# A seven-product scheme for the down product of seven turns, and weight sums made by GpSimd in the middle stage

## The reference

```python
D_MODEL = 1024
D_FF = 4 * D_MODEL
    xn = rmsnorm(x, norm1_g)
    proj = xn @ w_in
    ...
    mixed = jax.nn.sigmoid(gate_a) * y_a + jax.nn.sigmoid(gate_b) * y_b
    h = x + mixed @ w_o
    f = jnp.square(jax.nn.relu(rmsnorm(h, norm2_g) @ w_up)) @ w_down
    return h + f, new_buf_a, new_buf_qkv, S_new
```

## Time and profile before

| what | value |
|---|---|
| median of 3 runs | 1758.71 us (1756.45 to 1761.66) |
| profiled execution, span | 1754.7 us |
| TensorE busy | 1725.3 us, 98% |
| VectorE busy | 993.6 us, 57% |
| ScalarE busy | 566.7 us, 32% |
| GpSimd busy | 124.1 us, 7% |
| mean granted TensorE clock | 0.996 |
| DMA | 126.48 MB, mean 72 GB/s |

### The profile page before, as it was taken

One profiled execution on the slowest core, in us unless ns is written; L12 is line 12 of the kernel. 1 busy time (PEld: TensorE's weight loads), 2 busy tenths in 40 slices (PEclk: granted clock), 3 DMA queues, 4 the chain that ended last, 5 costly groups with the idle time before them and its releaser, 6 DMA issues.

```text
span 1754.7 us, 25319 instructions
## 1 busy us (share of the span) xinstructions
PE 1725.3 (98%) x10557; PEld 1620.3 (92%) x10557; DVE 993.6 (57%) x1457; ACT 566.7 (32%) x1134; POOL 124.1 (7%) x109
## 2 busy tenths in 40 slices
PE   6999999999999999999999999999999999999998
PEld 6999989998999999999988899999998888999987
DVE  5566547665411142322162877777789666667667
ACT  5222224444211111111141544444344232333334
POOL 1000023433000000000000300000002000000001
PEclk9999999999999999999999999999999999999999
DMA  6011111000511111021060133333333212232313
GB/s 195 25 39 46 54 43 48 1 25 27 167 37 49 37 37 49 25 61 49 13 240 1 57 109 108 101 97 96 97 96 97 86 59 73 84 97 84 96 61 120
DMA packets 119757, 126.48 MB, mean 72 GB/s; under 512 B 5178, under 2 KB 96007, under 8 KB 119644
## 3 DMA queue, kind: packets, MB, share of 16 engines
q1 hardware_dynamic: 119644, 124.87, 23.0%
HBM read 115.21 MB, written 9.64 MB: 71 GB/s over the span
## 4 chain that ended last, share of the span: by engine, by line
PE 82%; DVE 3%; issue 1%; ACT 1%; POOL 0%; POOLq 0%; DVEq 0%; ACTq 0%
PE ps L1898 26%; PE ps L2697 21%; PE ps L2685 20%; PE ps L2634 6%; PE ps L1381 2%; PE ps L1404 1%; PE ps L1462 0%; PE ps L1477 0%; PE ps L1486 0%; PE ps L1440 0%; PE ps L1320 0%; PE ps L1471 0%; DVE ft L1136 0%; PE ps L2646 0%; DVE ti L1168 0%
## 5 line engine op out<-in xcount | busy, mean ns | idle before, releaser
L2697 PE MATMUL ps<-w_hi,hid_hi 128*128 128x512 f32 x576 | 224.6, 390 | 1.4 <-DVE rows L2476 1.4
L1898 PE MATMUL ps<-xn_hi,g_hi 128*128 128x384 f32 x672 | 225.0, 335 | 0.0
L1898 PE MATMUL ps<-xn_lo,g_hi 128*128 128x384 f32 x672 | 224.5, 334 | 0.0
L1898 PE MATMUL ps<-xn_hi,g_lo 128*128 128x384 f32 x672 | 224.5, 334 | 0.0
L2697 PE MATMUL ps<-w_hi,hid_lo 128*128 128x512 f32 x576 | 224.3, 389 | 0.0
L2697 PE MATMUL ps<-w_lo,hid_hi 128*128 128x512 f32 x576 | 224.1, 389 | 0.0
L2685 PE MATMUL ps<-x_half,w_hi 128*128 128x320 f32 (+1 forms) x832 | 193.8, 303 | 0.3 <-DVE xn_hi L2420 0.3
L2476 DVE TENSOR_TENSOR rows<-ps,rows 128x512 f32<-128x512 f32 x144 | 99.3, 690 | 121.2 <-PE ps L2697 120.9
L2177 ACT CAST w_hi<-ff_raw 128x1024 fp32r<-128x1024 f32 x112 | 116.6, 1055 | 141.7 <-PE ps L2697 141.7
L2685 PE MATMUL ps<-x_half,w_lo 128*128 128x320 f32 (+1 forms) x512 | 154.9, 302 | 0.0
L2378 DVE TENSOR_TENSOR w_lo<-ff_raw,w_hi 128x1024 fp32r<-128x1024 f32 x112 | 136.6, 1220 | 31.4 <-ACT w_hi L2177 30.5
(11 more groups left out here) (308 smaller groups left out, 3367.3 us busy)
## 6 DMA issues: line engine op xcount, KB each, us to landing
ff_raw<-in_w_up SPq DMA_DIRECT2D x64, 512.0 KB, 4.4
ff_raw<-in_w_down SPq DMA_DIRECT2D x32, 512.0 KB, 3.7
s<-in_w_down SPq DMA_DIRECT2D x32, 512.0 KB, 3.6
g_raw<-in_w_in SPq DMA_DIRECT2D x28, 512.0 KB, 3.8
w_raw<-in_w_in SPq DMA_DIRECT2D x16, 512.0 KB, 3.9
rows<-in_x_prompt SPq DMA_DIRECT2D x9, 512.0 KB, 6.4
wo_raw<-in_w_o SPq DMA_DIRECT2D x8, 512.0 KB, 3.7
out<-out SPq DMA_DIRECT2D x8, 512.0 KB, 2.6
```

What stands on the lines that cost most here:

```text
L1898: last = nc.tensor.matmul(ps[:, ORDER[n % 8], 0:NW], a[:, u % 3, w], x[:, c, rows_of(g)], start=(c == 0 and m == 0), stop=(c == ks - 1 and ...
L2697: last = nc.tensor.matmul(ps[:, 6 + n % 2, :], x[:, k, at], y[s][:, w], start=(first and k == ks[0] and m == 0), stop=((not first or len(k ...
```

## The change

In turns 8 to 14, that is seven turns of the second row group (`squeezed`), the down product is a seven-product scheme too. The hidden block of 640 rows is taken as 256 rows on top, one middle tile of 128 rows and 256 rows below. Top and bottom are multiplied in seven products (`DOWNS`), each of two tiles x 6 matmuls of 512 columns; the middle tile is plain, four pieces of 6 matmuls (`middle_row`). VectorE makes four sums of hidden blocks (`hidden_sum`), and nine remainders of forms (`rest_form`) in place of eight of blocks. Products that belong to several outputs stay in their PSUM bank, and the next is summed on top of them after the bank has been added to `rows`: 16 additions (`evict`) in place of 10, and TensorE waits for an addition before it goes on in that bank. Turn 15 and the first group keep the plain down product. The weights of these turns are eight units in place of four, four of them sums of quarters of w_down (T1 to T4).

`weight_sum` is gone from all turns. The sums of w_up quarters (S1 to S4) and of w_down quarters are made once, for both groups, in the middle stage: 32 sets (`SETS`), for each of which SyncE loads four pieces of 256 KB into ff_piece (`prep_load`), GpSimd makes four sums in place, each waiting for the one before (`prep_sums`), and SyncE stores the four results in DRAM (`prep_store`, ff_sums). The pieces are single buffers: the loads of a set wait for the stores of the one before. One set is stored and one loaded in each pass of the loop that loads the units of the middle stage. The feed-forward loads are one ring of five slots (`load_unit`), in the order in which the units are used, 11 a turn and 15 in the seven turns, in place of 8. Joins, squarings, copies and casts of hidden blocks are done two blocks at a time.

```diff
--- before.py
+++ after.py
+        prep = [self.at("ff_piece", [P, 512], F32, self.mem.spare + n * 2048) for n in range(4)]
+        self.ff_sums = nc.dram_tensor("ff_sums", [NFC, 8, P, D], F32).ap()
+        prep_in, prep_out, before_prep = z_in[1], z_in[0], 32
...
+        def prep_load(sp, n):
+            c, down, half = n // 4, n // 2 % 2, n % 2
+            if n:
+                sp.wait_ge(prep_out, before_prep + 64 * n)
+            else:
+                sp.wait_ge(self.rule.wx_done, H)
+                for f in range(2):
+                    sp.wait_ge(z_in[f], before_prep)
+            for j, piece in enumerate(prep):
+                row, col = divmod(j, 2)
+                if down:
+                    sp.dma_start(piece[:, :], down_view[:, 4 * c + 2 * row + half, col * 512:(col + 1) * 512]
...
+        def prep_store(sp, n):
+            c, down, half = n // 4, n // 2 % 2, n % 2
+            sp.wait_ge(prep_made, 4 * n + 4)
+            for piece, j in zip(prep, (0, 2, 3, 1) if down else (1, 3, 2, 0)):
+                sp.dma_start(self.ff_sums[c, 4 * down + j, :, half * 512:(half + 1) * 512], piece[:, :]
+                             ).then_inc(prep_out, 16)
+
+        def prep_sums(pool, n):
+            p11, p12, p21, p22 = [piece[:, :] for piece in prep]
+            tensor = nc.gpsimd.tensor_tensor
+            pool.wait_ge(prep_in, before_prep + 64 * n + 64)
+            if n // 2 % 2:
+                tensor(p11, p12, p11, ALU.subtract).then_inc(prep_made, 1)
+                pool.wait_ge(prep_made, 4 * n + 1)
+                tensor(p12, p22, p12, ALU.subtract).then_inc(prep_made, 1)
+                pool.wait_ge(prep_made, 4 * n + 2)
+                tensor(p22, p22, p11, ALU.subtract).then_inc(prep_made, 1)
+                pool.wait_ge(prep_made, 4 * n + 3)
...
             for u in range(3, NU):
                 load(sp, u)
+                if u >= 4:
+                    prep_store(sp, u - 4)
+                if u < 3 + SETS:
+                    prep_load(sp, u - 3)
...
             sp.wait_ge(tails_stored, 32)
+            sp.wait_ge(prep_out, before_prep + 64 * SETS)
             closing.sync(sp)
         def gpsimd(pool):
+            for n in range(SETS):
+                prep_sums(pool, n)
             closing.gpsimd(pool)
...
+        UPS = ("U11", "U12", "S2", "S1", "S3", "S4", "U22")
+        UD = len(UPS)
+        plain = ("B11", "B21", "B12", "B22")
+        squeezed = lambda t: NFC <= t < TURNS - 1
+
+        DOWNS = (("a11", "B11"), ("s1", "T1"), ("s2", "T2"), ("a12", "B21"), ("s3", "T3"), ("s4", "B22"), ("a22", "T4"))
+        squeezed_units = (("B11", "T1", "T2", "B21", "T3", "B22", "T4"),
+                          ("B11", "T1", "T2", "B21", "T3", "B22", "B12", "T4"))
...
+        ff_at = (t0 + 24576, t0 + 28672, t0 + 8192, t0 + 20480, spare + 4096)
+        SLOTS = len(ff_at)
...
+        ROW = {"B11": 0, "T1": 1, "T2": 0, "B21": 0, "T3": 1, "B22": 0, "T4": 1}
+        COL = {"B11": 0, "T1": 1, "T2": 1, "B21": 0, "T3": 1, "B22": 1, "T4": 0}
+        DOWN_BANK = {"B11": 6, "T1": 0, "T2": 6, "B21": 2, "T3": 6, "B22": 0, "T4": 6}
+        FRESH = ("B11", "T1", "B21")
...
+            def load_unit(t, j):
+                n, name, c = number(t, j), kinds(t)[j], t % NFC
+                if n >= SLOTS:
+                    sp.wait_ge(lo_done, NU + n - SLOTS + 1)
...
-            def weight_sum(t, n):
-
-                tensor = nc.vector.tensor_tensor
-                if n == 1:
-                    dve.wait_ge(raw_ready[0], 32 + 16 * (2 * t + 1))
-                    dve.wait_ge(raw_ready[1], 32 + 16 * (t + 1))
...
+            def hidden_sum(t, n):
...
+                if n == 1:
+                    dve.wait_ge(relu_sq, squares_of(t) + 3)
+                    ins = tensor(s1, a21, a22, ALU.add)
+                if n == 2:
+                    dve.wait_ge(form_sum, sums_made(t) + 1)
+                    ins = tensor(s2, s1, a11, ALU.subtract)
+                if n == 3:
+                    ins = tensor(a21, a11, a21, ALU.subtract)
+                if n == 4:
+                    dve.wait_ge(form_sum, sums_made(t) + 2)
+                    dve.wait_ge(kept_squared, squeezed_before(t) + 1)
+                    ins = tensor(s4, a12, s2, ALU.subtract)
...
                 rest(t, UD + 1)
+                if squeezed(t):
+                    g = group(t)
+                    join(t, 2)
+                    relu_square(t, 2)
+                    for n in (1, 2, 3):
+                        hidden_sum(t, n)
+                    rest_form(t, "s1")
+                    rest_form(t, "a22")
+                    hidden_sum(t, 4)
+                    rest(t, UD + 2)
+                    if g:
+                        rest_form(t, "mid0")
+                    rest_form(t, "s2")
+                    evict_pair(t, "B11")
+                    evict_pair(t, "T1")
+                    rest(t, UD + 3)
+                    rest_form(t, "a12")
+                    if g:
+                        rest_form(t, "mid1")
+                    evict_pair(t, "T2")
+                    rest(t, UD + 4)
+                    rest_form(t, "s3")
+                    rest_form(t, "s4")
+                    rest(t, UD + 5)
+                    evict_pair(t, "B21")
+                    if g:
+                        evict(t, "mid", 1)
+                        evict_pair(t, "T3")
+                        rest(t, UD + 6)
+                        rest(t, UD + 7)
+                        evict_pair(t, "B22")
+                        rest(t + 1, 0)
+                        evict(t, "mid", 3)
+                    else:
+                        evict_pair(t, "T3")
+                        rest(t, UD + 6)
+                        evict_pair(t, "B22")
+                        rest(t + 1, 0)
+                    rest(t + 1, 1)
+                    evict_pair(t, "T4")
+                    continue
                 rest_hidden(t, 1)
                 join(t, 2)
...
+            def down_product(t, form_name, name):
+                weights_split(t, name)
+                form_split(t, form_name)
+                if name == "B11":
+                    pe.wait_ge(summed, sums(t))
+                if name == "T1":
+                    pe.wait_ge(joined, 3 * t + 3)
+                for x in range(2):
+                    if name in ("T2", "T3", "T4"):
+                        pe.wait_ge(summed, evicted(t, {"T2": "B11", "T3": "T2", "T4": "T3"}[name], x))
+                    if name == "B22":
+                        pe.wait_ge(summed, evicted(t, "T1", x))
+                    down_piece(t, form_name, name, x, DOWN_BANK[name] + x, name in FRESH, True)
+
+            def middle_row(t, n):
+
+                name, k = (("B11", 0), ("B21", 1), ("B22", 1), ("B12", 0))[n]
+                weights_split(t, name)
+                form_split(t, f"mid{k}")
+                if n == 0:
+                    pe.wait_ge(kept, 4 * t + 4)
+                down_piece(t, f"mid{k}", name, 0, 4 + n // 2, n % 2 == 0, n % 2 == 1)
 
 
...
+                if squeezed(t):
+                    for form_name, name in DOWNS:
+                        down_product(t, form_name, name)
+                        if group(t) and name in ("T1", "B21"):
+                            middle_row(t, int(name == "B21"))
+                        if group(t) and name == "B22":
+                            middle_row(t, 2)
+                            middle_row(t, 3)
```

More of the change, by code:

```diff
@@ new lines, in close @@
+        two = lambda *names: [(n, x) for n in names for x in range(2)]
+        PIECES = (two("B11", "T1", "T2", "B21", "T3", "B22", "T4"),
+                  two("B11", "T1") + [("mid", 0)] + two("T2", "B21") + [("mid", 1)] + two("T3", "B22") +
+                  [("mid", 2), ("mid", 3)] + two("T4"))
+        EVICTS = [[x for x in pieces if x not in (("mid", 0), ("mid", 2))] for pieces in PIECES]
+        FREED = ({n: (n, 1) for n in squeezed_units[0]},
+                 {**{n: (n, 1) for n in squeezed_units[1]}, "B11": ("mid", 0), "B21": ("mid", 1), "B22": ("mid", 2),
+                  "B12": ("mid", 3)})
@@ L1949, in close @@
+        kinds = lambda t: UPS + (squeezed_units[group(t)] if squeezed(t) else plain)
+        first_unit = [0]
+        for t in range(TURNS):
+            first_unit.append(first_unit[-1] + len(kinds(t)))
+        TOTAL = first_unit[TURNS]
+        number = lambda t, j: first_unit[t] + j
         unit = lambda t, j: NU + number(t, j)
+        index = lambda t, name: kinds(t).index(name)
         slot = lambda t, j: number(t, j) % 4
-        downs = lambda t: sum(2 * tiles_of(n) for n in range(t))
@@ L1954, in close @@
-        ff_at = (t0 + 24576, t0 + 28672, t0 + 8192, t0 + 20480)
-        r21, r22, r12, r11 = [unit_at("ff_raw", F32, a) for a in ff_at]
-        pieces = lambda a: a[:, :].rearrange("p (k c) -> p k c", c=512)
-        s1 = self.at("s1", [P, 2, 800], F32, const + 5120)[:, :, 0:512]
-        s2 = self.at("s2", [P, 2, 8704], F32, base + 53248)[:, :, 0:512]
```

(8 more changed lines are left out.)

392 lines of the change are left out of this document (228 added, 164 removed).

## The result

The changed kernel takes 1869.7 us (median of four runs, 1863.3 to 1878.7), against 1757.6 us for the kernel before (median of four, 1753.5 to 1761.7): a ratio of 1.065, with a 95% interval of 1.061 to 1.069. It is slower, as forecast, but by twice the forecast amount: 1813.3 us was the prediction and 1852 us its upper end. Measured again beside later runs, the ratio was 1.059 (1.055 to 1.062). All ratios are of fast executions; the only one left out for its state is an execution of 3434.4 us of the later run without sums. The profiled execution took 1863.3 us, with a span of 1860.6 us.

The account below looks back on a forecast made before the run. TensorE's own time was taken as the bound. Span 1754.7 + 75.0 (set chain) - 19.0 (seven turns) - 1.4 (turn 7) = 1809.3 us; the median, 4.0 us above the span, gives 1813.3 us, range 1764 to 1852 us.

Parts of the forecast that it names:

- one chain of 32 T: Middle stage: 32 sets in sequence on SyncE's queue, w_o loaded only after the last store; shift 75.0 us.
- T: Middle stage: cycle of one set, loads landed, sums made, stores landed; 15.3 us predicted, no shift at 12.96 us.
- Rival (c): Middle stage: more GpSimd-VectorE meetings or slower landings, T = 16.6 us, 1855 us; chance 11%.
- the landing of the four loads: Middle stage: 1 MB of a set in four loads of 256 KB lands in mean 5.1 us.
- The bounds: Parts of a set's cycle: loads 3.6 to 5.7 us, stores 3.6 to 5.4, sums 4.4 to 7.8; together 11.7 to 19.0.
- The stores: Middle stage: a set's four stores land in 3.9 us, 2.7 for half and 1.3 for the other half.
- The sums and the lock: Middle stage: four GpSimd sums 5.3 us a set, plus 0.9 us for meetings with VectorE's two-input SBUF instructions.
- The seven turns: Turns 8 to 14: twelve fewer matmuls each, 2.72 us a turn, 19.0 us in all; VectorE 40.1 of 49.1 us.
- rival (d): Turns 8 to 14 don't get shorter because VectorE's strict order holds TensorE up: 1832 us; chance 5%.
- Turn 7: Removed weight sums end TensorE's waits for late additions of the down product there: 1.4 us gained.
- The signs named in advance: Trace signs: sets 15.3 us apart, first w_o load about 948 us, g_lo waits about 65 us, turns 49.1 us apart.
- The rival on the other side: Middle stage: the sets fit, T at or under 12.96 us, giving 1738.3 us, faster; chance 6%.

Follow-up runs that it names:

- the later run without sums: Changed kernel with GpSimd's sums removed, each set's four pieces loaded and stored again unsummed ("no sums" in the table): 1738.6 us, ratio 0.989.
- late weight load: Changed kernel, but the next unit's 512 KB weight load is issued only when the set's four loads have landed: 1822.8 us, ratio 1.040.
- one buffer, fewer requests: Changed kernel with late weight load, w_down sets loaded by one request and every set stored by one: 1813.8 us, ratio 1.033.
- plain down product: Changed kernel with sets still made, but all turns of the second row group take the plain down product: 1880.2 us, ratio 1.073.
- two buffers: Changed kernel with each set cut into two halves of 256 columns, a buffer each in the same 8 KB: 1748.8 us, ratio 0.997.
- two buffers, fewer requests: Kernel of two buffers with two loads and one store per half set instead of four and four: 1734.4 us, ratio 0.989.

## Why the prediction was wrong in size

**The place and the mechanism were right.** The prediction put the whole loss in one chain of 32 T on SyncE's queue, with its formula: 1738.3 us plus 32 (T - 12.96). With the T that each run shows, it gives:

| kernel | T, us | by the formula | measured |
|---|---|---|---|
| changed kernel | 16.90 | 1864 | 1869.7, 1860.3 |
| late weight load | 15.66 | 1825 | 1822.8 |
| one buffer, fewer requests | 15.27 | 1812 | 1813.8 |
| plain down product | 16.81 | 1862 + 18.4 = 1880 | 1880.2 |
| two buffers | 13.38 | 1752 | 1748.8 |
| two buffers, fewer requests | 12.27 | 1738 | 1734.4 |
| no sums | 11.74 | 1738 | 1738.6 |

Within 6 us in each (under T = 12.96 us the formula gives 1738 us throughout). So what failed is T: 16.9 against 15.3 us, 32 x 1.6 = 51 us, which is what the spans differ by from the forecast (105.9 against 54.6). That these agree so closely is in part luck: the first set started 3.8 us earlier than forecast, the fourth w_lo ended 1.5 us later behind the last store, and 2.4 us less were gained behind it. The other 5 us of the 56 between the medians is that the profiled execution was the fastest of its four. Rival (c), "more meetings, or landings like the slower ones", with T = 16.6 us and 1855 us, came nearest; it had 11%, and of its two reasons the landings were the right one.

**The step that failed: the landing of the four loads**, put at 5.1 us, was 6.1. I took it from two loads of 512 KB, with the next pair issued 2.7 us behind the first load, and added 0.5 us for the shorter runs of w_up. In the changed kernel loads of w_up and of w_down landed alike (6.10 and 6.18 us), and with the late weight load they were 0.2 us apart (5.90 and 5.68). The kernel before, behind the pair at 876.82 us:

```profile
879.54 1.50 SPq L2067 DMA_DIRECT2D wo_raw<-in_w_o  x2
```

Two parts of what was missing are shown. For w_down the same megabyte in four requests takes 0.5 us longer than in one (5.68 against 5.18 us on average), and the next unit's 512 KB, issued directly behind the set's loads (2.0 us after the first), adds 0.35 us (6.14 against 5.79). What stays open is why one request took 5.18 us where the two of the row took 4.8. The second part was in the code of the change for all to see: the prediction looked at what stands behind a wait in the queue, but not at what stands behind a transfer. The bounds named 5.7 us as the slow end, which was too low too: it came from a ratio of speeds, with no neighbour in it. The effect goes both ways; the weight loads land later as well (median us from issue to landing),'s loads in the kernel before against the kernel after:

```profile
g_raw<-in_w_in SPq DMA_DIRECT2D x26, 512.0 KB, 3.8
...
g_raw<-in_w_in SPq DMA_DIRECT2D x25, 512.0 KB, 5.6
```

**The stores**, put at 3.9 us, took 4.05 to 4.10 us in 23 of 32 sets, but 4.3 to 6.2 us in the other nine, 4.40 us on average. What tells the nine from the others is in the DMA view of each set's stores: beside all nine, and beside none of the 23, runs one transfer of 8 or 16 KB on a queue that the profile calls instruction. The window of the stores that took 5.93 us (587.68 to 593.61 us), then that of stores that took 4.06 us (605.57 to 609.63 us), each with packets, MB and the share of the 16 engines:

```profile
q1 hardware_dynamic: 576, 1.05, 48.1%
q8 instruction: 1, 0.02, 1.0%
```

```profile
q1 hardware_dynamic: 576, 1.05, 69.4%
```

With the late weight load it is the same: 22 sets without such a transfer store in 4.05 to 4.09 us, ten with one in 4.08 to 5.93 us. Loads beside one land later too, in the changed kernel 6.45 us on average in nine sets against 6.02 in 23. The two always stand side by side, but that they are cause and effect is not shown: no run moves or removes these transfers. Together, 1.0 and 0.5 us a set are 49 of the 51 us.

On the price of one transfer the Trainium skill, page "DMA: Bandwidth & Descriptors", section "Anatomy of one DMA — SWDGE (gpsimd) path", gives a fit for requests issued by GpSimd: 2.0 us and the bytes at 436 GB/s; worked out from it, an estimate for 1 MB is 4.4 us. No run here issues from GpSimd. Here SyncE issues, and one request took 4.1 us as a store and 5.1 us as a load; a group of four loads, with a neighbour, took 6.1 us.

**The sums and the lock** were right in size: 5.3 + 0.9 = 6.2 us predicted, 6.24 measured, and 5.37 where the phase removes the meeting. The reason given was half right. Once the loads are late, the remainder does always fall into the sums; but it costs GpSimd one wait of 0.87 us a set, by phase, not 1.3 meetings, and the long sums are 2.13 to 2.31 us, not 2.5.

**The seven turns**: 2.63 us each, 2.72 predicted; 18.4 against 19.0 us. VectorE was at 39.8 of 49.2 us (40.1 predicted), and TensorE waited for nothing there: rival (d) is out. Turn 7 went from 43.97 to 42.10 us, 1.9 us against the 1.4 predicted.

**The signs named in advance**: the first w_o load at about 948 us came at 995.9, by the same T, though the first set started 3.8 us earlier; waits for g_lo of about 65 us in the middle stage came as 29 us for g_lo and 48 us for what follows from it, 81 us with one unexplained 4.1. The shift from w_o's first matmul on was to be no larger, and it did grow: it is 118.0 us at that matmul (889.11 to 1007.15 us) and 126.1 us at the first turn. Two things make this. TensorE waited 3.6 us for the fourth w_lo (the second wait of L2810 above). That is VectorE's order, not a slower load: from the end of the first w_lo to that of the fourth it takes 14.4 us, 14.3 before, but before, TensorE came to w_o 9.6 us behind the first w_lo, and now 3.9 us. The forecast's sum had this, since it took the shift at the fourth w_lo. And behind the wait TensorE ran at its lower level, 1.2 GHz, for 13 matmuls, 0.43 us apart where 0.227 us is the distance at 2.4 GHz:

```profile
1017.81:1023.50 5.69, 5.69 (x14) 4.43 (x15) 5.69 (x5) 4.18 (x4) 0.00 (x0) 0.50 0.31 92
```

These 5.69 us would have been 2.9 at the full clock. (The same happened to the first six matmuls of w_o, 1.4 us lost; 3.6 + 2.7 + 1.4 us are 7.7 of the 8.0 by which the shift grew.) The 2.7 us lost lie behind the fourth w_lo and are the 2.4 us by which the gain from there on, 18.0 us, stays under the 20.4 forecast: the turns themselves gave 18.4 + 1.9 = 20.3 us. The forecast had no term for the clock.

**Two slips of the text** change nothing: "one second of the load stretch" is one microsecond of it, and T = 13.8 us gives 1765 us by its own formula, not 1764.

**The rival on the other side** was worth its numbers. "The change pays down to T = 13.6 us" fits the two-buffer kernels: with 13.4 us the time is 0.3% under the kernel before, with 12.3 us 1.1% under. No run lies just above 13.6 us; the nearest, with 15.3 us, is 3.3% over.

## What to carry to other kernels

Work that is put on an idle engine is not free if a shared, in-order queue has to serve it: compare the period of the whole round trip (load, compute, store, each waited for) with the period of the loop that it is laid into, not the engine's busy time. If the round trip is longer, two half-size buffers in the same memory helped far more here than the two trimmings of its parts that were tried (13.4 us against 15.7 and 15.3, from 16.9), and then the number of requests counted, 0.47 us each. Giving the sets' requests to another engine's queue, so that no weight load stands behind them, was not tried. Price a transfer from a row with the same number of requests, in which as much stands directly behind it as will stand there after the change.
